# Moving columns of 256 and 512 in pairs of 64-byte lines: another order inside each matmul of a two-layer block

## The chip, the core and the metric

The kernel runs on one core of one Trainium2 chip. The metric is the device time of one execution in microseconds, from the first to the last of the core's work. Engines are named as in the profile: PE is TensorE's matmuls, PEld its loads of the stationary operand (weight loads), DVE is VectorE, ACT is ScalarE, POOL is GpSimd, SP issues most of the transfers.

## What is computed

Two transformer-like layers run one after the other on 256 tokens of width 2048, in float32. The first has sparse attention and a gated linear recurrence side by side, with 16 tokens put in front (so 272 rows); the second has a long convolution and grouped attention side by side, and then a feed-forward part of width 5632. Cut to what matters here:

```python
# first layer, 272 rows
proj = rms_norm(x, norm_g) @ w_in                      # 2048 -> 12,368
merged = sum_n(sigmoid(gates_n) * (y_n @ w_branch_n))  # attention and recurrence
x = x + merged @ w_out
# second layer, 256 rows
proj = rms_norm_2(x, mix_norm_g) @ w_in
merged = g_h * (y_h @ w_br_hyena) + g_a * (y_a @ w_br_attn)
x = x + merged @ w_out
h2 = rms_norm_2(x, ffn_norm_g)
return x + (silu(h2 @ w_ffn_gate) * (h2 @ w_ffn_up)) @ w_ffn_down
```

Nearly all of the arithmetic is in these products with weight matrices, which are read once each (393 MB from memory).

## The kernel before

**Splitting.** Products are made in a reduced float32 form (`float32r`). To keep float32's accuracy each operand is split in two parts, high and low, and a product is three matmuls: high by high, high by low, low by high. A weight matrix comes from memory in units into `raw`; ScalarE rounds half a unit into `w_hi` (L815, 128 x 1024 elements) and VectorE makes the rest, `w_lo = raw - w_hi` (L1348). Both have four slots; TensorE counts `half_done` when it has used a half, and ScalarE waits for that before it overwrites a slot. TensorE waits for `split_hi` and `split_lo` ahead of each half.

**Two shapes of product.** Activations are kept transposed, features on the partitions and tokens along the row. In `by_tile` (L2278) a tile of 128 x 128 weights is the stationary operand and a row of tokens moves: 256 columns of `x1t`, `hf_hi`/`hf_lo`, `yh`, `ya_hi`/`ya_lo`, or 272 columns of `h_hi`/`h_lo` in the first layer. Its matmuls are at L2285 (high weights) and L2290 (low weights). In `chunk` (L2330) and in the down projection (L2969 on, `down_step`) 128 tokens are stationary and 512 columns of `w_hi` or `w_lo` move: these matmuls are in `by_high` (L2275, L2276), at L2359 and at L2976; the very first and very last steps use `product` (L2269 to L2271). The page prints the operands as `ps<-moving,stationary`.

**Where things lie.** A row of 256 float32 columns is 1024 bytes, one of 512 is 2048, one of 272 is 1088. The kernel has constants `LINE, PHASE = 256, 64` (L126) and starts `x1t`, `hf_hi`, `hf_lo`, `y_hi`, `y_lo`, `yh`, `ya_hi`, `ya_lo`, `st_hi` and `st_lo` at an address that is 64 more than a multiple of 256; `w_hi`, `w_lo` and `h_hi` start at 128 more than a multiple of 256. Each result of a matmul of 512 columns fills a bank of PSUM (2 KB of each partition), one of 256 columns half a bank. ScalarE and VectorE read the banks in plain order.

**Order.** Each engine's program is written out by hand, with semaphores between. TensorE runs through the projections, puts the small products of attention, recurrence and convolution in between at fixed steps, and ends with the feed-forward part (L2285 and L2290 with `hf`, 1447 to 1945 us) and the down projection (L2275, L2276, L2976 with `st`, 1945 to 2191 us). One group of small matmuls matters for the prediction: L2568 multiplies by `half_blocks(ql, lev)`, which takes every second block of n = 1, 2, 4, ... 64 columns of a row of 128 (L557), so 64 columns in pieces of n, and writes them side by side.

Of the kernel before, what the change touches and what calls it, by code (L numbers as in the profile page):

```python
# [24 lines left out]
T = 256  # L25
# [38 lines left out]
def hybrid_layers(nc, a, out):  # L64

    ctx = ExitStack()
    with ctx:
# [2196 lines left out]
        @block.tensor  # L2264
        def _(pe):
            def product(dst, left, w_h, w_l, first, last):

                hi, lo = left
                pe.matmul(dst, hi, w_h, start=first, stop=False)  # L2269
                pe.matmul(dst, hi, w_l, start=False, stop=False)  # L2270
                return pe.matmul(dst, lo, w_h, start=False, stop=last)  # L2271

            def by_high(dst, left, w_h, first):

                pe.matmul(dst, left[0], w_h, start=first, stop=False)  # L2275
                pe.matmul(dst, left[1], w_h, start=False, stop=False)  # L2276

            def by_tile(q, h, k0, moving, dsts, last):  # L2278

                pe.wait_ge(split_hi, 8 * q + h + 1)  # L2280
                for e in range(4):
                    for x in range(2):
                        w_h = w_hi[:, h % 4, e // 2, (e % 2) * T + x * P:(e % 2) * T + (x + 1) * P]
                        for i, part in enumerate(moving(k0 + e)):
                            pe.matmul(dsts[x], w_h, part, start=(k0 + e == 0 and i == 0), stop=False)  # L2285
                pe.wait_ge(split_lo, 8 * q + h + 1)
                for e in range(4):
                    for x in range(2):
                        w_l = w_lo[:, h % 4, e // 2, (e % 2) * T + x * P:(e % 2) * T + (x + 1) * P]
                        ins = pe.matmul(dsts[x], w_l, moving(k0 + e)[0], start=False, stop=(k0 + e == last))  # L2290
                ins.then_inc(half_done, 1)
# [38 lines left out]
            def chunk(q, halves, left, dsts, width=W, step=None, new=None, fresh=False):  # L2330

                n = 2 * len(halves)
                for x, h in enumerate(halves):
# [15 lines left out]
                    else:  # L2349
# [6 lines left out]
                        for e in range(2):  # L2356
                            k = 2 * x + e
                            for i, dst in enumerate(dsts):
                                ins = pe.matmul(dst, left(k, i)[0], w_lo[:, h % 4, e, 0:width],  # L2359
                                                start=False, stop=(k == n - 1))  # L2360
# [608 lines left out]
            def down_step(k, par, h, s, outs, first, last):  # L2969
# [5 lines left out]
                for bank, e, cols in outs:  # L2975
                    ins = pe.matmul(ps[bank][:, :], st_hi[:, par, s, cols], w_lo[:, h % 4, e, :], start=False, stop=last)  # L2976
                ins.then_inc(half_done, 1)
# [111 lines left out]
```

## Time and profile before

| | us |
|---|---|
| time, median of 2 runs | 2197.01 (2196.88 to 2197.14) |
| span of the profiled execution, first to last instruction | 2195.1 |
| time around the span (median less span) | 1.9 |
| TensorE matmuls busy | 2188.4, 14295 instructions |
| weight loads busy | 1978.1, 14295 instructions |
| VectorE, ScalarE, GpSimd busy | 1374.6, 1000.1, 359.0 |

The profiled execution has no time of its own beside its span. The page gives the busy time of each engine, then the span in slices, then the chain of work that ended last, followed back from the end. A group of instructions is one line of the kernel with one operation and one pair of operands; behind the bar stand the time in which at least one of the group ran, the mean duration of one in ns, and the idle time of the engine just before. Matmuls overlap in the records, so a duration is longer than the time from one start to the next.

### The profile page before, as it was taken

How to read it: one execution, taken by the hardware profiler on the slowest of the kernel's cores; microseconds unless marked ns; L12 is line 12 of the kernel's file. 1: busy time of each engine (PE TensorE's matmuls, PEld its weight loads, DVE VectorE, ACT ScalarE, POOL GpSimd, SP SyncE). 2: the span in 40 equal slices, each digit the busy share in tenths (PEclk: the TensorE clock that was granted, in tenths of full speed). 3: DMA queues.
4: the chain of work that ended last, by engine and by line, in shares of the span. 5: the costliest groups of instructions: out<-in, count | busy, mean ns of one | idle time of the engine just before them, and what ended most of it. 6: DMA issues, size and time to landing. Idle time of an engine off the chain costs nothing.

```text
span 2195.1 us, 34712 instructions
## 1 busy us (share of the span) xinstructions
PE 2188.4 (100%) x14295; PEld 1978.1 (90%) x14295; DVE 1374.6 (63%) x1873; ACT 1000.1 (46%) x1328; POOL 359.0 (16%) x437
## 2 busy tenths in 40 slices
PE   9999999999999999999999999999999999999999
PEld 7898889988888878899999999899999999988887
DVE  6777557968575576677775546555555555554444
ACT  6446544253444446555544444454344333444443
POOL 6563999760000000000000000000000000000000
PEclk9999999999999999999999999999999999999999
DMA  8655556444465645554455556555555555555553
GB/s 274 196 168 176 181 172 189 145 154 153 154 212 198 214 156 171 171 182 145 157 189 173 192 173 194 190 186 182 189 190 179 185 191 183 182 190 192 178 190 129
DMA packets 276530, 396.63 MB, mean 181 GB/s; under 512 B 9399, under 2 KB 198162, under 8 KB 270896
## 3 DMA queue, kind: packets, MB, share of 16 engines
q1 hardware_dynamic: 272704, 384.52, 53.4%
q0 software_dynamic: 3648, 10.37, 1.8%
q8 instruction: 81, 1.33, 0.2%
q14 instruction: 33, 0.27, 0.0%
q10 hardware_dynamic: 64, 0.14, 0.0%
HBM read 392.91 MB, written 2.10 MB: 180 GB/s over the span
## 4 chain that ended last, share of the span: by engine, by line
PE 98%; DVE 1%; DMA 0%; ACT 0%; SPq 0%; issue 0%; DVEq 0%
PE ps L2285 32%; PE ps L2290 16%; PE ps L2275 15%; PE ps L2276 15%; PE ps L2359 11%; PE ps L2976 4%; PE ps L2568 1%; PE ps L2318 0%; PE ps L2515 0%; DMA raw<-w_in 0%; PE ps L2475 0%; PE ps L2791 0%; PE ps L2851 0%; PE ps L2811 0%; PE ps L2837 0%; PE ps L2724 0%
## 5 line engine op out<-in xcount | busy, mean ns | idle before, releaser
L1348 DVE TENSOR_TENSOR w_lo<-raw,w_hi 128x1024 fp32r<-128x1024 f32 x719 | 893.7, 1250 | 630.4 <-ACT w_hi L815 624.6
L815 ACT ACTIVATE w_hi<-raw 128x1024 fp32r<-128x1024 f32 x719 | 751.3, 1057 | 732.2 <-PE ps L2290 446.3
L2285 PE MATMUL ps<-hf_hi,w_hi 128*128 128x256 f32 x1408 | 339.4, 281 | 0.0
L2285 PE MATMUL ps<-hf_lo,w_hi 128*128 128x256 f32 x1408 | 339.1, 281 | 0.0
L2285 PEld LDWEIGHTS ps<-hf_lo,w_hi 128*128 128x128 f32 x1408 | 266.4, 189 | 0.1
L2285 PEld LDWEIGHTS ps<-hf_hi,w_hi 128*128 128x128 f32 x1408 | 265.8, 189 | 0.1
L2275 PE MATMUL ps<-w_hi,h_hi 128*128 128x512 f32 x572 | 232.9, 407 | 0.6 <-DVE h_lo L1403 0.6
L2285 PE MATMUL ps<-x1t,w_hi 128*128 128x256 f32 x1792 | 232.1, 282 | 0.0
L2276 PE MATMUL ps<-w_hi,h_lo 128*128 128x512 f32 x572 | 224.8, 393 | 0.0
L2285 PEld LDWEIGHTS ps<-x1t,w_hi 128*128 128x128 f32 x1792 | 218.5, 189 | 1.9 <-issue 1.4
L2290 PE MATMUL ps<-hf_hi,w_lo 128*128 128x256 f32 x1408 | 194.3, 281 | 0.0
L2290 PEld LDWEIGHTS ps<-hf_hi,w_lo 128*128 128x128 f32 x1408 | 178.1, 189 | 0.0
L2359 PE MATMUL ps<-w_lo,h_hi 128*128 128x512 f32 x572 | 155.3, 393 | 0.0
L2275 PE MATMUL ps<-w_hi,st_hi 128*128 128x512 f32 x348 | 138.3, 397 | 0.0
L2276 PE MATMUL ps<-w_hi,st_lo 128*128 128x512 f32 x348 | 138.3, 397 | 0.0
L2359 PEld LDWEIGHTS ps<-w_lo,h_hi 128*128 128x128 f32 x572 | 107.4, 188 | 24.7
L2275 PEld LDWEIGHTS ps<-w_hi,h_hi 128*128 128x128 f32 x572 | 107.5, 188 | 23.3 <-DVE h_lo L1403 0.8
L2276 PEld LDWEIGHTS ps<-w_hi,h_lo 128*128 128x128 f32 x572 | 107.8, 188 | 21.8
L2290 PE MATMUL ps<-x1t,w_lo 128*128 128x256 f32 x896 | 123.0, 280 | 0.0
L2290 PEld LDWEIGHTS ps<-x1t,w_lo 128*128 128x128 f32 x896 | 112.9, 189 | 0.0
L2285 PE MATMUL ps<-h_hi,w_hi 128*128 128x272 f32 x384 | 100.7, 295 | 0.0
L2285 PE MATMUL ps<-h_lo,w_hi 128*128 128x272 f32 x384 | 98.4, 288 | 0.0
(512 smaller groups left out, 3122.4 us busy)
## 6 DMA issues: line engine op xcount, KB each, us to landing
raw<-w_in SPq DMA_DIRECT2D x163, 1024.0 KB, 5.2
raw<-w_ffn_gate SPq DMA_DIRECT2D x44, 1024.0 KB, 5.1
raw<-w_ffn_up SPq DMA_DIRECT2D x44, 1024.0 KB, 5.1
raw<-w_ffn_down SPq DMA_DIRECT2D x44, 1024.0 KB, 4.9
raw<-w_out SPq DMA_DIRECT2D x32, 1024.0 KB, 5.1
raw<-w_branch SPq DMA_DIRECT2D x16, 1024.0 KB, 5.1
raw<-w_br_hyena SPq DMA_DIRECT2D x8, 1024.0 KB, 5.8
raw<-w_br_attn SPq DMA_DIRECT2D x8, 1024.0 KB, 5.8
```

The lines of the kernel that those rows point to most:

```text
L815: act.activation(w_hi[:, h % 4, :, 0:width], raw[:, h // 2, 2 * (h % 2):2 * (h % 2) + 2, 0:width], ACT.Copy).then_inc(split_hi, 1)
L1348: dve.tensor_tensor(w_lo[:, h % 4, :, 0:width], raw[:, h // 2, 2 * (h % 2):2 * (h % 2) + 2, 0:width], w_hi[:, h % 4, :, 0:width].bitcast(F ...
L2275: pe.matmul(dst, left[0], w_h, start=first, stop=False)
L2276: pe.matmul(dst, left[1], w_h, start=False, stop=False)
L2285: pe.matmul(dsts[x], w_h, part, start=(k0 + e == 0 and i == 0), stop=False)
L2290: ins = pe.matmul(dsts[x], w_l, moving(k0 + e)[0], start=False, stop=(k0 + e == last))
L2359: ins = pe.matmul(dst, left(k, i)[0], w_lo[:, h % 4, e, 0:width], start=False, stop=(k == n - 1))
L2568: ins = pe.matmul(ps[6 + c][0:rows, i * (P // 2):(i + 1) * (P // 2)].rearrange("p (k n) -> p k n", n=2 ** (lev - 1)), kl[:, i, c * P:c * P ...
L2976: ins = pe.matmul(ps[bank][:, :], st_hi[:, par, s, cols], w_lo[:, h % 4, e, :], start=False, stop=last)
```

## The change

TensorE's matmuls read a row of 256 or 512 moving columns in another order and write their results in the same order, so each result lands where it did before. A row is cut in two halves and each half in pieces of 16 columns (64 bytes); piece 0 of the first half is followed by piece 0 of the second half, then come piece 1 of both, and so on to the last pair. Inside a piece the order is plain. The two pieces of a pair are 512 bytes apart for 256 columns, 1024 bytes for 512. It is done by an access pattern of three dimensions (pair, half, column) in place of one, on the moving operand and on the result; stationary operands, instructions, waits and transfers stay. Rows of any other length (the 272 of the first layer, the narrow ones) are left as they were: `sweep` returns them unchanged.

```diff
+            def sweep(x):
+
+                return x.rearrange("p (a j s) -> p j a s", a=2, s=16)[:, :, :, :] if x.shape[1] in (T, W) else x
+
             def product(dst, left, w_h, w_l, first, last):
 
                 hi, lo = left
+                dst, w_h, w_l = sweep(dst), sweep(w_h), sweep(w_l)
                 pe.matmul(dst, hi, w_h, start=first, stop=False)
...
             def by_high(dst, left, w_h, first):
 
+                dst, w_h = sweep(dst), sweep(w_h)
                 pe.matmul(dst, left[0], w_h, start=first, stop=False)
                 pe.matmul(dst, left[1], w_h, start=False, stop=False)
...
                         for i, part in enumerate(moving(k0 + e)):
-                            pe.matmul(dsts[x], w_h, part, start=(k0 + e == 0 and i == 0), stop=False)
+                            pe.matmul(sweep(dsts[x]), w_h, sweep(part), start=(k0 + e == 0 and i == 0), stop=False)
...
-                        ins = pe.matmul(dsts[x], w_l, moving(k0 + e)[0], start=False, stop=(k0 + e == last))
+                        ins = pe.matmul(sweep(dsts[x]), w_l, sweep(moving(k0 + e)[0]), start=False, stop=(k0 + e == last))
...
-                                ins = pe.matmul(dst, left(k, i)[0], w_lo[:, h % 4, e, 0:width],
+                                ins = pe.matmul(sweep(dst), left(k, i)[0], sweep(w_lo[:, h % 4, e, 0:width]),
                                                 start=False, stop=(k == n - 1))
...
-                    ins = pe.matmul(ps[bank][:, :], st_hi[:, par, s, cols], w_lo[:, h % 4, e, :], start=False, stop=last)
+                    ins = pe.matmul(sweep(ps[bank][:, :]), st_hi[:, par, s, cols], sweep(w_lo[:, h % 4, e, :]),
+                                    start=False, stop=last)
```

## Rows read from the trace of the kernel before

**Rows 1.** The page: busy time, granted TensorE clock by slice, chain by engine.
```profile
PE 2188.4 (100%) x14295; PEld 1978.1 (90%) x14295; DVE 1374.6 (63%) x1873; ACT 1000.1 (46%) x1328; POOL 359.0 (16%) x437
...
PEclk9999999999999999999999999999999999999999
...
PE 98%; DVE 1%; DMA 0%; ACT 0%; SPq 0%; issue 0%; DVEq 0%
```
**Rows 2.** Waits of TensorE, longest first: us in total, times, longest us.
```profile
PE ps L2420 <- DVE junk L1394: 1.5, 1, 1.5
```
**Rows 3.** Groups by line, PE, 1600 to 1650 us: count | busy us, mean ns | idle.
```profile
L2285 PE MATMUL ps<-hf_lo,w_hi 128*128 128x256 f32 x144 | 34.7, 281 | 0.0
L2285 PE MATMUL ps<-hf_hi,w_hi 128*128 128x256 f32 x144 | 34.7, 281 | 0.0
L2290 PE MATMUL ps<-hf_hi,w_lo 128*128 128x256 f32 x139 | 19.5, 281 | 0.0
```
**Rows 4.** The same view of 1456 to 1471 us.
```profile
L2285 PE MATMUL ps<-hf_lo,w_hi 128*128 128x256 f32 x46 | 10.7, 276 | 0.0
L2285 PE MATMUL ps<-hf_hi,w_hi 128*128 128x256 f32 x46 | 10.7, 276 | 0.0
L2290 PE MATMUL ps<-hf_hi,w_lo 128*128 128x256 f32 x43 | 5.9, 276 | 0.0
```
**Rows 5.** The same view of 2000 to 2050 us.
```profile
L2276 PE MATMUL ps<-w_hi,st_lo 128*128 128x512 f32 x72 | 28.6, 397 | 0.0
L2275 PE MATMUL ps<-w_hi,st_hi 128*128 128x512 f32 x72 | 28.6, 397 | 0.0
L2976 PE MATMUL ps<-w_lo,st_hi 128*128 128x512 f32 x72 | 19.8, 397 | 0.0
```
**Rows 6.** Line L2276 alone: durations min/median/max in ns, first and last start.
```profile
L2276 PE MATMUL ps<-w_hi,h_lo x572: 387/393/403, 12.8 to 718.0; 128*128 128x512 f32 x191
...
L2276 PE MATMUL ps<-w_hi,st_lo x348: 397/397/398, 1945.1 to 2187.3; 128*128 128x512 f32 x174
...
L2276 PE MATMUL ps<-w_hi,x1t x224: 387/392/398, 848.7 to 1445.9; 128*128 128x512 f32 x112
```
**Rows 7.** Line L2290 alone, in the same columns.
```profile
L2290 PE MATMUL ps<-hf_hi,w_lo x1408: 276/281/281, 1448.8 to 1944.8; 128*128 128x256 f32 x176
...
L2290 PE MATMUL ps<-h_hi,w_lo x384: 283/288/296, 118.1 to 442.3; 128*128 128x272 f32 x192
```
**Rows 8.** Groups by line over the whole span, PE, one row of each pattern.
```profile
L2285 PE MATMUL ps<-hf_hi,w_hi 128*128 128x256 f32 x1408 | 339.4, 281 | 0.0
...
L2275 PE MATMUL ps<-w_hi,h_hi 128*128 128x512 f32 x572 | 232.9, 407 | 0.6 <-DVE h_lo L1403 0.6
L2285 PE MATMUL ps<-x1t,w_hi 128*128 128x256 f32 x1792 | 232.1, 282 | 0.0
...
L2275 PE MATMUL ps<-w_hi,st_hi 128*128 128x512 f32 x348 | 138.3, 397 | 0.0
...
L2290 PE MATMUL ps<-x1t,w_lo 128*128 128x256 f32 x896 | 123.0, 280 | 0.0
...
L2275 PE MATMUL ps<-w_hi,x1t 128*128 128x512 f32 x224 | 88.7, 396 | 0.0
```
**Rows 9.** Timeline, PE, around 391, 423 and 439 us: start, us, xcount.
```profile
390.14 1.28 PE L2568 MATMUL ps<-ql,kl 128*128 128x64 f32 x10
...
422.08 1.28 PE L2568 MATMUL ps<-ql,kl 128*128 128x64 f32 x10
...
438.21 1.15 PE L2568 MATMUL ps<-ql,kl 128*64 128x64 f32 x16
```
**Rows 10.** Line L2837 alone: plain float32, 512 columns, the slowest here.
```profile
L2837 PE MATMUL ps<-zt,t_cos x8: 590/592/595, 1059.7 to 1087.0; 128*128 128x512 f32 x8
```
**Rows 11.** Groups by line, all engines, 1600 to 1650 us: the two splitters.
```profile
L1348 DVE TENSOR_TENSOR w_lo<-raw,w_hi 128x1024 fp32r<-128x1024 f32 x18 | 22.0, 1225 | 23.1 <-ACT w_hi L815 22.9
...
L815 ACT ACTIVATE w_hi<-raw 128x1024 fp32r<-128x1024 f32 x18 | 19.1, 1059 | 30.9 <-PE ps L2290 30.9
```

## The prediction

> **What bounds the kernel now.** I read the page first. TensorE is busy for the whole span, its granted clock is full in every slice, and the chain of work that ended last is 98% TensorE [rows 1]. The view of waits then shows that TensorE hardly waits: its largest wait is 1.5 us in total [rows 2]. So the time is the number of matmuls times the pace at which they follow one another, and nothing else has to be late for a change of that pace to show in full.
>
> The pace can't be read off the duration in a group, because a record's end is modelled; it has to be counted. A view of one stretch counts every matmul that touches it, so those begun up to one duration before it come off. In 50 us of the feed-forward part there are 144 + 144 + 139 = 427 records of 281 ns, less 2.4 for the edge: 50/424.6 = 117.8 ns [rows 3]. In another stretch the same instructions show 276 ns and 46 + 46 + 43 = 135 records in 15 us: 15/132.6 = 113.1 ns [rows 4]. In the down projection there are 3 x 72 = 216 records of 397 ns in 50 us: 233.3 ns [rows 5]. Record less pace is 163 ns all three times. From here on I read the pace of any steady group as its duration less 163.
>
> At 2.4 GHz, the granted level, 256 columns alone would be 106.7 ns and 512 columns 213.3 ns. So a matmul of 256 loses 11 ns, one of 512 some 17 ns (229 to 233), though no wait is recorded. That loss is what an order of columns could touch.
>
> What sets it? Three observations. The same instruction runs at 276 or 281 and keeps to it for long stretches [rows 3, 4]. With the same moving tile, `w_hi`, a matmul of 512 shows 392 or 393 where the weights loaded meanwhile are of `x1t` or `h_lo` and 397 where they are of `st_lo` [rows 6], so the loading of the next weights has a part in it. And where rows start 64 bytes further round each time (the 272 columns of `h_hi` are 1088 bytes, against the 256 bytes that the kernel's LINE names), records spread from 283 to 296; rows of 256 columns, which all start at the same place, show 276 to 281 [rows 7]. I read this as two readers, the moving stream and the load of the next weights, that get in each other's way depending on which 64-byte line of four each is at. That reading is an inference; no view shows a collision.
>
> **The change part by part.** Nothing is added or removed: the same matmuls, weight loads, waits and transfers. Only the order changes in which columns are read and results written. Matmuls of 256 columns that go the new way: 3 x 1408 with `hf`, 1792 + 896 with `x1t`, and 768 with `yh` and `ya`: 7680. Of 512 columns: 3 x 572, 3 x 348, 3 x 224, 6 x 128 with `y` and `hf`, and 24 at the first and last steps: 4224 [rows 8], which has one row of each pattern. The 272-column ones stay. That is 7680 x 117.6 = 903 us and 4224 x 230.6 = 974 us, 1877 of the span of 2195.1. In pieces of 16 columns it is 122,880 + 135,168 = 258,048 jumps.
>
> *A jump in reading.* The matmuls at L2568 already read broken rows: at the first level 64 columns come as 64 pieces of one column, at the fifth as 4 pieces of 16. Both go at (1.28 - 0.27)/9 = 112 ns; at the last level 64 columns in one piece, with half the weights, go at 62 ns or less [rows 9]. So 112 ns is the pace of loading 128 weights, and 64 jumps hide in the 50 ns between: a jump costs at most 0.8 ns, at least nothing. Over all pieces the upper end is 206 us. I take nothing, since 60 jumps more make no difference between the two levels.
>
> *A jump in writing.* No matmul of the trace writes a broken row of PSUM, so nothing prices it from a row nearby. The bound below is nothing, as each piece is 16 results side by side. The bound above is the slowest 512 columns here: 592 - 163 = 429 ns, 1.9 times the pace now [rows 10]. I take nothing, because the broken reads showed nothing. The Trainium skill speaks against that: "Advanced Engine Details and Errata", section Memory Cachelines, says that any non-contiguous pattern in PSUM slows matmuls significantly, but also that two neighbours side by side give the best throughput, which pieces of 16 satisfy. By its first sentence the time would be that of the fourth rival below, by its second nothing is lost.
>
> *The meeting with the weight load.* A weight load passes 512 bytes, eight 64-byte lines, in 112 ns: 14 ns a line. The moving stream now passes one in 117.8/16 = 7.4 ns, twice as fast, so the two meet at changing places. With pairs 512 or 1024 bytes apart, both whole multiples of 256, the stream stays two pieces long at each of the four places and then goes on: 14.7 ns a place, the speed of the load. If both walk the same way they keep in step and hardly meet; if the load runs the other way round, they meet for longer each time. No row tells the direction. From below, the quickest paces that rows show: 113.1 for 256 and 387 - 163 = 224 for 512 [rows 4, 6], a gain of 7680 x 4.5 + 4224 x 6.6 = 35 + 28 = 63 us; if all loss went, 256 would still stand at the load's 112 ns and 512 at 213.3, a gain of 43 + 73 = 116 us. From above, meeting twice as often doubles the loss: 7680 x 11 + 4224 x 17.3 = 84 + 73 = 157 us. Between such ends I take the steady paces that rows show at mixed places. The 272 rows at 288 - 163 = 125 ns are 117.6 for 256 columns, today's pace; the few stretches that run quick now lose 4.5 ns, some 450 matmuls, 2 us; 512 goes to the steady 233.3, which costs the 3180 matmuls that aren't of the down projection 3.6 ns each, 11 us. Sum: +13 us.
>
> *What lies behind TensorE.* If it got quicker the splitters would have to keep up. In the 50 us of the feed-forward part VectorE splits 18 halves in 22.0 us and waits 23.1 us for ScalarE, which itself waits 30.9 us for TensorE [rows 11]. Both have room for 5%, so a gain would not be eaten there.
>
> The sum goes on the span, 2195.1 us; the median, 2197.0, has 1.9 us around it. 2197 + 13 = 2210 us, +0.6%.
>
> **Rivals.** *In step:* the stream and the load walk the same way and the pace falls to the quick one. For it: 276-ns records exist and last [rows 4]. Against it: the start of rows is already laid out (LINE, PHASE), and the direction is unknown. 2197 - 63 = 2134 us; it decides from 256 at 114.5 and 512 at 226 on. This ends on the other side, faster by over 2%.
>
> *Against the load:* the two walk opposite ways and each meeting lasts longer. For it: the spread of 13 ns in the 272 rows [rows 7] shows that places alone can cost that much. Against it: whoever is held up once is out of step with the other for a while. Half the doubled loss is 79 us, 2276 us; all of it 2354. It decides once 256 takes over 121 ns and 512 over 236.
>
> *No difference at all:* the order inside a row does not matter, the loss being per 64-byte line whatever line comes next (11 ns is 16 lines x 0.7). Then 2197 us; it falls in the same band as my forecast.
>
> *Broken writes are slow:* matmuls go at the 429 ns per 512 columns of rows 10, 1.9 times the pace. 1877 x 0.87 = 1630 us more, about 3830 us. Nothing in the rows speaks for it.
>
> **How the numbers follow.** 2% of 2197 is 44 us, about what a measurement of this kernel can tell from no change. About the same, with no difference included (2153 to 2241): 0.42. In step, faster: 0.20. Against the load, slower: 0.33. Slow writes: 0.05. So faster 0.20, same 0.42, slower 0.38. The forecast is the likeliest, 2210 us, with 2153 to 2241 as its own range. For 8 in 10 the range takes in the whole middle, the in-step case at the paces that rows already show (2134, so down to 2130), and the against case up to about three quarters of the doubled loss (2197 + 113 = 2310). Outside stay a full loss removed (2081), the loss doubled and the slow writes.
>
> **What would show it.** The page after must again be 98% TensorE in its chain, with the full clock and as many matmuls; else a step has become a wait that I don't see. Records of 256 columns near 281 to 283 and of 512 near 397 bear out the sum. 276 and 387 or less are in step; 284 and over with 400 and over is against the load; 600 and over for 512 columns is slow writes. The 272-column rows, which don't change, must stay at 283 to 296: if they move too, it isn't the order. If 256 and 512 move in opposite ways, the reading with two walkers is right in kind and my price for one of them wrong. I would be wrong in kind if the weight loads, 188 ns now, grew: then it is the load that is held up and not the stream.

## The result: slower, 2254.44 us, and the profile after

The changed kernel takes 2254.44 us (median of 2 runs, 2254.37 to 2254.52) against 2197.01: ratio 1.0261 [1.0242, 1.0279]. That is 57 us more where the prediction had 13 more, inside its wide range and outside the likeliest case's own (2153 to 2241).

The page after: busy times, the clock by slice and the chain by engine, which answer to [rows 1].

```profile
PE 2246.4 (100%) x14295; PEld 2009.5 (89%) x14295; DVE 1375.1 (61%) x1873; ACT 1001.2 (44%) x1328; POOL 352.7 (16%) x437
...
PEclk9999999999999999999999999999999999999999
...
PE 99%; DVE 0%; DMA 0%; ACT 0%; SPq 0%; issue 0%; DVEq 0%
```

As many matmuls, the same clock, still a chain of matmuls alone. No wait was added: the matmuls themselves follow one another more slowly. Groups by line, PE only, in 50 us of the feed-forward part (1650 to 1700) and of the down projection (2050 to 2100); they answer to [rows 3] and [rows 5] (the change moved the lines by 6).

```profile
L2291 PE MATMUL ps<-hf_hi,w_hi 128*128 128x256 f32 x142 | 34.9, 284 | 0.0
L2291 PE MATMUL ps<-hf_lo,w_hi 128*128 128x256 f32 x141 | 34.6, 283 | 0.0
L2296 PE MATMUL ps<-hf_hi,w_lo 128*128 128x256 f32 x136 | 19.1, 283 | 0.0
...
L2281 PE MATMUL ps<-w_hi,st_hi 128*128 128x512 f32 x71 | 28.6, 402 | 0.0
L2282 PE MATMUL ps<-w_hi,st_lo 128*128 128x512 f32 x70 | 28.2, 402 | 0.0
L2982 PE MATMUL ps<-w_lo,st_hi 128*128 128x512 f32 x69 | 19.5, 402 | 0.0
```

142 + 141 + 136 = 419 matmuls of 256 columns, less 2.4 for the edge, are 50/416.6 = 120.0 ns; 71 + 70 + 69 = 210 of 512 columns, less 1.7, are 50/208.3 = 240.0 ns. Record less pace is still 163. The single lines, minimum/median/maximum in ns, which answer to [rows 6] and [rows 7]:

```profile
L2282 PE MATMUL ps<-w_hi,h_lo x572: 402/403/407, 12.8 to 735.9; 128*128 128x512 f32 x191
L2282 PE MATMUL ps<-w_hi,st_lo x348: 402/402/403, 1995.6 to 2244.7; 128*128 128x512 f32 x174
L2282 PE MATMUL ps<-w_hi,x1t x224: 402/402/407, 871.6 to 1485.9; 128*128 128x512 f32 x112
...
L2296 PE MATMUL ps<-hf_hi,w_lo x1408: 282/284/289, 1489.1 to 1995.2; 128*128 128x256 f32 x176
...
L2296 PE MATMUL ps<-h_hi,w_lo x384: 283/288/296, 121.4 to 450.2; 128*128 128x272 f32 x192
```

Three things are to be seen. The 272 columns, which the change leaves alone, stand where they stood, so it is the order. The 512 columns of `h_lo`, `st_lo` and `x1t`, which differed before (393, 397, 392), are now all alike. And the new paces are round: 120.0 is 106.7 + 16 x 0.83 and 240.0 is 213.3 + 32 x 0.83, as much as if every 64-byte line of a moving row cost 0.83 ns, one cycle of 1.2 GHz, above the bare columns.

Counted from the starts of all matmuls in the two traces, the changed ones of 256 columns took 906.0 us before and 926.2 after, those of 512 columns 989.0 and 1026.3, everything else 294.6 and 294.6. The two differences, 20.3 and 37.3, are the 57.5 us by which the span grew.

### The profile page after: what moved, and what is told of

The parts are those of the page before. It is cut to its first block, busy times and chain, and to the rows that moved or that the text cites. A ratio compares the mean times of both kernels' runs of the same rounds, so it can differ in the third digit from the quotient of the medians.

```text
span 2252.6 us, 34712 instructions
## 1 busy us (share of the span) xinstructions
PE 2246.4 (100%) x14295; PEld 2009.5 (89%) x14295; DVE 1375.1 (61%) x1873; ACT 1001.2 (44%) x1328; POOL 352.7 (16%) x437
## 4 chain that ended last, share of the span: by engine, by line
PE 99%; DVE 0%; DMA 0%; ACT 0%; SPq 0%; issue 0%; DVEq 0%
PE ps L2291 31%; PE ps L2296 16%; PE ps L2281 15%; PE ps L2282 15%; PE ps L2365 11%; PE ps L2982 4%; PE ps L2574 1%; PE ps L2324 0%; PE ps L2521 0%; DMA raw<-w_in 0%; PE ps L2481 0%; PE ps L2857 0%; PE ps L2797 0%; PE ps L2817 0%; PE ps L2843 0%; PE ps L2730 0%
## 5 line engine op out<-in xcount | busy, mean ns | idle before, releaser
L2291 PE MATMUL ps<-hf_hi,w_hi 128*128 128x256 f32 x1408 | 345.9, 284 | 0.0
L2291 PE MATMUL ps<-hf_lo,w_hi 128*128 128x256 f32 x1408 | 345.4, 283 | 0.0
L2281 PE MATMUL ps<-w_hi,h_hi 128*128 128x512 f32 x572 | 237.9, 416 | 0.6 <-DVE h_lo L1403 0.6
L2291 PE MATMUL ps<-x1t,w_hi 128*128 128x256 f32 x1792 | 237.7, 286 | 0.0
L2282 PE MATMUL ps<-w_hi,h_lo 128*128 128x512 f32 x572 | 230.4, 403 | 0.0
L2291 PEld LDWEIGHTS ps<-x1t,w_hi 128*128 128x128 f32 x1792 | 223.8, 190 | 1.9 <-issue 1.4
L2365 PE MATMUL ps<-w_lo,h_hi 128*128 128x512 f32 x572 | 160.5, 403 | 0.0
```

The lines of the kernel that those rows point to most:

```text
L2291: pe.matmul(sweep(dsts[x]), w_h, sweep(part), start=(k0 + e == 0 and i == 0), stop=False)
L2365: ins = pe.matmul(sweep(dst), left(k, i)[0], sweep(w_lo[:, h % 4, e, 0:width]), start=False, stop=(k == n - 1))
```

## The experiments

### Results apart from reads

Which half of the change costs: `sweep` stays on the moving operand alone, or on the result alone.

```diff
-                dst, w_h = sweep(dst), sweep(w_h)
+                dst, w_h = plain(dst), sweep(w_h)        # reads only; plain(x) returns x
+                dst, w_h = sweep(dst), plain(w_h)        # writes only
...
```

Reads only:

> Only the moving operand is read in pairs; results are written in plain order (so columns of each product change places, which alters the values but not the work). Theory A and B (reading is what costs): 120 and 240 ns, about 2254 us. Theory C (writing costs): the paces of before, 113 to 118 and 226 to 233, about 2197 us.

Writes only:

> Only the results are written in pairs; the moving operand is read in plain order (columns of each product change places, the work is the same). Theory A and B: the paces of before, about 2197 us. Theory C (writing costs): 120 and 240 ns, about 2254 us.

Reads only took 2254.42 us, ratio 1.0261 [1.0240, 1.0281]; writes only 2196.96 us, ratio 0.9999 [0.9989, 1.0009]. Groups by line of the kernel that only writes in the new order (1650 to 1700 and 2050 to 2100 us, one row of each):

```profile
L2295 PE MATMUL ps<-hf_hi,w_hi 128*128 128x256 f32 x142 | 34.3, 281 | 0.0
...
L2286 PE MATMUL ps<-w_hi,st_lo 128*128 128x512 f32 x72 | 28.6, 397 | 0.0
```

281 and 397 are the records of the kernel before [rows 3, 5]. The whole price is in the read; 64-byte pieces half a row apart cost nothing when written to PSUM.

### Other orders, same pieces

The first edit takes the pairs from the last to the first, the second exchanges neighbouring pieces (1, 0, 3, 2, ...); both keep every jump.

```diff
-                return x.rearrange("p (a j s) -> p j a s", a=2, s=16)[:, :, :, :] ...
+                return x.rearrange("p (a j s) -> p j a s", a=2, s=16)[:, ::-1, :, :] ...    # last to first
+                return x.rearrange("p (j a s) -> p j a s", a=2, s=16)[:, :, ::-1, :] ...    # neighbours
```

> The same pairs, taken from the last pair to the first; inside a piece of 16 columns the order stays plain. The changed kernel shows 120.0 ns for 256 columns and 240.0 for 512, that is 0.83 ns over the streaming time for every piece of 16, whatever weights are loaded. Theory A (a jump has a fixed price of 0.83 ns, wherever it goes and whatever the weight load does): 120 and 240 again, about 2254 us. Theory B (the stream walks against the weight load): turned round it walks with it, the meetings go, 256 columns fall to 112 to 114 ns and 512 to 214 to 226, so 2050 to 2140 us. Theory C (the broken writes cost it): as A, about 2254 us.

> Another order with a jump after every piece: the row goes in pieces of 16 columns with neighbours exchanged (1, 0, 3, 2, ...), so successive pieces never share their place modulo 256 bytes. Theory A (fixed price of a jump): 120 and 240 ns, about 2254 us. Theory D (the price is for two pieces in succession at the same place modulo 256 bytes): paces like those before the change, 113 to 118 and 226 to 233, 2140 to 2200 us. Theory B (against the load): somewhere between the two, with a spread over matmuls that the flat 240 of the changed kernel doesn't have.

From last to first took 2188.84 us, ratio 0.9963 [0.9949, 0.9977]: quicker than the changed kernel and than the kernel before. Neighbours exchanged took 2234.96 us, 1.0172 [1.0155, 1.0189]. Groups by line in the down projection (2050 to 2100 us) and the feed-forward part (1650 to 1700), first from last to first, then neighbours exchanged:

```profile
L2282 PE MATMUL ps<-w_hi,st_lo 128*128 128x512 f32 x74 | 28.8, 389 | 0.0
...
L2291 PE MATMUL ps<-hf_lo,w_hi 128*128 128x256 f32 x142 | 34.2, 280 | 0.0
```

```profile
L2282 PE MATMUL ps<-w_hi,st_lo 128*128 128x512 f32 x71 | 28.3, 398 | 0.0
...
L2291 PE MATMUL ps<-hf_lo,w_hi 128*128 128x256 f32 x142 | 34.9, 284 | 0.0
```

As many jumps, backward, are free: from start to start the 512 columns with `st` follow one another at 228 ns, under the 233 of before, those of 256 at 117. (389 less 163 would be 226: between orders the difference of record and pace moves by some 2 ns.) So there is no fixed price of a jump. Theory D falls as well: neighbours exchanged never put two pieces at the same place one after the other, and yet 256 columns went at 120.0 ns, where 113 to 118 were expected, and 512 with `st` at 235.5. Direction counts, as the theory of two walkers said, but the size it gave (2050 to 2140 us) was far off: the 256 columns gained nothing (906.0 us in all, as before), the 512 columns 8.3 us. Whether the load of weights had any part in it was left to the next runs.

### Is it the load of the next weights?

Some matmuls load only 32 of their 128 stationary columns: the second moving part of every product, and the low ones that don't close a sum. This is done to the changed order, the plain order and the order from last to first.

```diff
-                pe.matmul(dst, left[1], w_h, start=False, stop=False)
+                pe.matmul(dst[0:32], left[1][:, 0:32], w_h, start=False, stop=False)
```

> The changed kernel's order, but the matmuls of the second moving part, and the low matmuls that don't close a sum, load only 32 of their 128 stationary columns (and so fill 32 of 128 result rows: this part of the computation is left out); the moving columns are as many as before. The load that lies beside a matmul is then a quarter as long wherever the next matmul is one of these. Theory Load (the 0.83 ns per 64-byte piece comes from the moving read meeting the load of the next weights): beside a short load 256 columns fall from 120 to 107 to 110 ns and 512 from 240 to 213 to 222; beside a full load they stay 120 and 240. Theory Order alone (the pieces of the forward order cost 0.83 ns each whatever the load does): 120 and 240 beside short and full loads alike.

> The order of the kernel before, with the same matmuls cut to 32 stationary columns (the same part of the computation left out). Theory Load: the loss of the plain order is of the same kind, so beside a short load 256 columns fall from 113 to 118 to about 107 to 110 ns, and 512 from 229 to 233 to 213 to 218. Theory Order alone, with the plain order's loss coming from the read too: 113 to 118 and 229 to 233 as in the kernel before. If the plain order falls and the forward pairs of e5 don't, the two losses are of different kinds.

> The pairs from last to first, as in e1, with the same matmuls cut to 32 stationary columns (the same part of the computation left out). Theory Load: beside a short load 107 to 110 and 213 to 218 ns, the same as the other two orders, since the order matters only through the load. Theory Order alone: 113 to 121 and 226 to 231 as in e1, and other than e5 by the same 2.6 and 11 ns as with full loads.

The times, one run each: changed order 2253.03, plain 2169.86, from last to first 2187.44 us, beside 2197.15 of the kernel before on the same chip. Groups by line of the changed order, 2050 to 2100 us, matmuls and then weight loads, and one row of 1650 to 1700:

```profile
L2281 PE MATMUL ps<-w_hi,st_hi 128*128 128x512 f32 x70 | 28.2, 403 | 0.0
L2282 PE MATMUL ps<-w_hi,st_lo 128*32 128x512 f32 x70 | 28.2, 403 | 0.0
...
L2281 PEld LDWEIGHTS ps<-w_hi,st_hi 128*128 128x128 f32 x69 | 13.1, 190 | 8.9
L2282 PEld LDWEIGHTS ps<-w_hi,st_lo 128*32 128x32 f32 x69 | 7.7, 112 | 3.4
...
L2292 PE MATMUL ps<-hf_hi,w_hi 128*128 128x256 f32 x138 | 33.9, 283 | 0.0
```

The load beside `st_hi`'s matmul, that of the next weights, took 191 ns in the changed kernel and takes 112 here, by the records; the matmul is at 403, against 402. The changed order pays its 0.83 ns a line beside the short load too: theory Load falls for it. The plain order in the same two stretches:

```profile
L2282 PE MATMUL ps<-w_hi,st_lo 128*32 128x512 f32 x72 | 28.4, 394 | 0.0
...
L2292 PE MATMUL ps<-hf_hi,w_hi 128*128 128x256 f32 x149 | 34.7, 277 | 0.0
```

Here the load has a share: 256 columns fall from 281 to 277, about 4 of the 11 ns that they lose (the quick stretches of [rows 4] stood at 276), 512 columns with `st` only from 397 to 394 to 396. The order from last to first hardly moved (2188.84 and 2187.44 us). So two things had been taken for one: a small share of the load, which the plain order of 256 columns has, and a loss of the read by itself, which stays without it.

### One walk backward, and pieces of other sizes

One walk from the last piece to the first; then pieces of 32 columns, forward and backward; pieces of 8; and even pieces before odd ones.

```diff
+                return x.rearrange("p (j s) -> p j s", s=16)[:, ::-1, :] ...                    # one walk backward
+                return x.rearrange("p (a j s) -> p j a s", a=2, s=32)[:, :, :, :] ...           # 128 bytes
+                return x.rearrange("p (a j s) -> p j a s", a=2, s=32)[:, ::-1, :, :] ...        # 128 bytes, backward
+                return x.rearrange("p (a j s) -> p j a s", a=2, s=8)[:, :, :, :] ...            # 32 bytes
+                return x.rearrange("p (j a s) -> p a j s", a=2, s=16)[:, :, :, :] ...           # even, then odd
```

> One walk instead of two: pieces of 16 columns, no pairs, from the last piece to the first, columns plain inside a piece, results written alike. Theory Load (the load runs against a forward read): a single walk backward runs the way of the load at twice its speed, meets it about a third as often as the plain order and stays longer: between the backward pairs and the plain order, 2180 to 2200 us, 256 columns 113 to 118, 512 columns 226 to 232. Theory Order alone, price for any piece that is not the next line forward: e1 already speaks against that, 2254 us. Theory Pairs (it is going back and forth between two halves that costs, the direction only in the change of half): about 2197 us.

> The order of the changed kernel with pieces of 32 columns (128 bytes) in place of 16. e5 to e7 showed that the price does not come from the weight load, so it lies in the order of reading alone. Theory Piece (the first 64 bytes of every piece wait one cycle of 1.2 GHz, 0.83 ns, what follows in line goes on at full pace): 256 columns are 8 pieces, 106.7 + 6.7 = 113.3 ns, 512 are 16, 213.3 + 13.3 = 226.7 ns; 2254 - 7680 x 6.7 - 4224 x 13.3 = 2147 us, below the kernel before. Theory Line (every 64-byte line pays in a pair order, however long the piece): 120 and 240, 2254 us. Theory Plain inside (inside a piece the plain order's own loss of about half a cycle a line, at its start one cycle): 256 columns 113.3 + 8 x 0.42 = 117 ns, 512 columns 226.7 + 16 x 0.5 = 235 ns, about 2205 us.

> Pairs of 128-byte pieces from last to first. Theory Piece: as the forward pairs of 128 bytes or quicker, 113 and 227 at most, 2147 us or less. Theory Line: as e1, 117 and 229, 2189 us. Theory Plain inside: between e1 and the kernel before, 2189 to 2197 us.

> Forward pairs of pieces of 8 columns (32 bytes), so that each 64-byte line is opened twice. Theory Piece: 256 columns are 32 pieces, 106.7 + 26.7 = 133.3 ns, 512 are 64, 266.7 ns; 2254 + 7680 x 13.3 + 4224 x 26.7 = 2469 us. Theory Line, where a line that was left can be returned to for nothing: 120 and 240, 2254 us. If the two lines of a pair hold each other up at each change: 266.7 and more.

> No pairs: first the even pieces of 16 columns from first to last, then the odd ones, so each piece starts 128 bytes after the one before, and never at the next line. Theory Piece: 120 and 240, 2254 us, as with the pairs. If only pieces that are a multiple of 256 bytes apart hold each other up (pairs, half a row apart): near the plain order or below, 113 to 118 and 227 to 233, 2147 to 2197 us.

| order | us | ratio | 256 columns, ns | 512 columns (`st_hi`), ns |
|---|---|---|---|---|
| one walk backward | 2223.47 | 1.0119 [1.0102, 1.0136] | 117.8 | 237.5 |
| pairs of 128 bytes | 2231.47 | 1.0155 [1.0138, 1.0172] | 118.8 | 238.0 |
| the same, backward | 2230.63 | 1.0151 [1.0134, 1.0168] | 118.7 | 237.1 |
| pairs of 32 bytes | 2279.65 | 1.0374 [1.0353, 1.0394] | 120.2 | 242.5 |
| even, then odd | 2264.81 | 1.0306 [1.0285, 1.0327] | 121.4 | 240.0 |

The paces are means from start to start with `hf` and `st_hi`; in pairs of 32 bytes other tiles of 256 columns took 121.7 to 125.0. Nearly all expectations missed. Pairs of 128 bytes have half the pieces and did not save half the price; 32 bytes have twice the pieces and cost 25 us more instead of 215. One walk backward is slower than either the plain order or the pairs backward. So it is neither a fixed price per piece, nor a fixed one per line, nor one of direction as such.

### The orders by themselves

Behind the last result of the kernel before, groups of 32 matmuls run with everything else idle, one group for each order, width, load and start; the `wide` row is that of `w_hi`.

```diff
             down_last(FKT // 4 - 1, 0)
+            pe.wait_ge(final_ready, 8)
+            for _ in range(32): pe.matmul(ps[0][:, 0:256], st_hi[:, 0, 0, 0:128], wide[:, 0:256], start=True, stop=True)
+            for _ in range(32): pe.matmul(ps[0][:, 0:256].rearrange(...), st_hi[:, 0, 0, 0:128], wide[:, 0:256].rearrange(...), ...)
...
```

> The kernel before, and behind its last result 84 groups of 32 more matmuls each, whose results nobody uses: one moving row of w_hi, one stationary tile of st_hi, while every other engine and nearly every transfer has ended. The groups go through twelve orders (plain; the changed kernel's; from last to first; neighbours exchanged; one walk backward; pairs of 128 bytes, forward and backward; pairs of 32 bytes; even pieces then odd; four walks forward and backward; both indices backward), 256 and 512 columns, 128 and 32 stationary columns, and for three orders other starts of the moving row and of the stationary tile, 64 bytes further each. The time is longer by the groups, 84 x 32 x about 180 ns = 480 us. Theory Order alone (the price lies in how the moving row is read, nothing else of the kernel takes part): the paces of the runs before: plain 113 to 118 and 226 to 233 ns, the changed order 120 and 240, from last to first 115 to 118 and 226 to 230, neighbours exchanged 120 and 235, pairs of 32 bytes 120 to 125 and 243, even then odd 121 and 240. Theory Traffic (ScalarE, VectorE and the transfers write the same memory meanwhile and hold the read up): with these idle all orders go at 107 to 110 and 213 to 218. Theory Load: equal paces of all orders beside 32 stationary columns only; e5 speaks against it. If the start of the row moves the pace of the plain or backward order, but not of the changed one, which 64-byte line of four is read when has a part in it.

The timeline of that part, PE: start in us, us from the first start to the last end, the line (one for each group). The rows are the plain order (L3011), the changed one (L3012) and that from last to first (L3013) for 256 columns, the same three for 512 columns (L3023 to L3025), and the plain and changed order of 256 columns beside 32 stationary columns (L3035, L3036).

```profile
2193.01 4.04 PE L3011 MATMUL ps<-w_hi,st_hi 128*128 128x256 f32 x32 [0.78 <-DVE x L2261]
2196.88 4.01 PE L3012 MATMUL ps<-w_hi,st_hi 128*128 128x256 f32 x32
2200.73 3.90 PE L3013 MATMUL ps<-w_hi,st_hi 128*128 128x256 f32 x32
...
2238.81 7.49 PE L3023 MATMUL ps<-w_hi,st_hi 128*128 128x512 f32 x32
2246.13 7.84 PE L3024 MATMUL ps<-w_hi,st_hi 128*128 128x512 f32 x32
2253.82 7.47 PE L3025 MATMUL ps<-w_hi,st_hi 128*128 128x512 f32 x32
...
2329.36 3.81 PE L3035 MATMUL ps<-w_hi,st_hi 128*32 128x256 f32 x32
2333.01 4.00 PE L3036 MATMUL ps<-w_hi,st_hi 128*32 128x256 f32 x32
```

A group's length less one record, over 31, is its pace: (4.01 - 0.283)/31 = 120.2 ns, (7.84 - 0.403)/31 = 239.9 ns. ScalarE, VectorE and the transfers have stopped, and the paces are those of the whole kernel within some 5 ns (the plain 512 columns with `st_hi` had 233.3 there and have 228.9 here), those of the changed order exactly: theory Traffic falls too. The time was 2670.42 us (one run), the groups included. Means from start to start within a group, the first few left out, with the moving row where it is and then 64, 128 and 192 bytes further:

| | 256 columns, ns | 512 columns, ns |
|---|---|---|
| changed order | 120.0, 120.3, 120.0, 120.0 | 240.0, 240.0, 240.0, 240.0 |
| plain | 117.8, 118.9, 113.5, 119.8 | 228.9, 233.2, 233.4, 227.5 |
| from last to first | 116.5, 116.7, 117.4, 120.7 | 228.3, 228.3, 226.7, 233.4 |

Other starts of the stationary tile moved the plain and the backward order in the same way (512 columns plain 226.8 to 233.4, backward 228.3 to 236.8) and the changed one not at all (120.0, 240.0 to 240.1). The plain order depends on the start: it pays as for half of its lines (113.3 = 106.7 + 8 x 0.83, 226.7 = 213.3 + 16 x 0.83) up to nearly all. The changed order always pays as for all. In no group, here or in the later runs, did the mean come below half. Beside 32 stationary columns the plain order of 256 columns goes at 113.3 here too; but with the moving row 128 bytes further it goes at 113.5 beside a full load as well, so what the load costs it depends on the start, and 512 columns gain nothing by the short load (231.1 against 228.9). Of the paces expected, those of neighbours exchanged were missed (117.8 and 233.3 in place of 120 and 235); one walk backward, for which none had been named, took 120.0 for 256 columns, against 117.8 in the kernel.

### Step and distance, one at a time

Again behind the kernel before: pieces of 16 columns at a fixed step of 1 to 8 lines, forward and backward, and pairs 16 to 32 lines apart, forward and backward.

```diff
+            for _ in range(24): pe.matmul(..., flat[:, 0:1024].rearrange("p (n d s) -> p n d s", n=16, s=16)[:, :, 0, :], ...)           # step 4
+            for _ in range(24): pe.matmul(..., flat[:, 0:544].rearrange("p (a j s) -> p j a s", a=2, s=16)[:, 0:8, :, :], ...)           # pairs 17 apart
```

> As the run of orders alone, with 120 groups of 24 matmuls behind the last result of the kernel before. A moving row is now 16 or 32 pieces of 16 columns out of all four slots of w_hi. Either each piece starts a fixed number of 64-byte lines after the one before (1 to 8, forward and backward), or pieces go in pairs that are 16, 17, 18, 19, 20, 24 or 32 lines apart, from the first pair on and from the last pair on; beside 128 and 32 stationary columns. Longer by 120 x 24 x about 180 ns = 520 us. Theory Same place (a piece waits for the one just before when both stand at the same of four 64-byte places of 256 bytes): steps of 4 and 8, either way, 120 and 240 ns or more; pairs 16, 20, 24 and 32 apart 120 and 240, pairs 17 and 19 apart less, 113 to 118 and 227 to 236. Theory Rhythm (which of four places stand where in the sequence decides, and order alone; nothing else of the distance): steps of 1, 5, -3 and -7 alike, -1, -5, 3 and 7 alike, 2 and 6 as even then odd, 120 and 240; pairs 16, 20, 24 and 32 apart alike. Theory Distance (any piece that is not the next line waits): every step but 1 at 120 and 240, pairs too, backward too; the runs from last to first speak against it.

The time was 2706.90 us (one run). Timeline rows of pairs 16, 17, 18, 19, 20, 24 and 32 lines apart, forward, 512 columns, 128 stationary columns (start, length):

```profile
2369.52 5.92 PE L3057 MATMUL ps<-w_hi,st_hi 128*128 128x512 f32 x24
2375.28 5.92 PE L3058 MATMUL ps<-w_hi,st_hi 128*128 128x512 f32 x24
2381.04 6.08 PE L3059 MATMUL ps<-w_hi,st_hi 128*128 128x512 f32 x24
2386.95 6.00 PE L3060 MATMUL ps<-w_hi,st_hi 128*128 128x512 f32 x24
2392.79 5.92 PE L3061 MATMUL ps<-w_hi,st_hi 128*128 128x512 f32 x24
2398.55 5.92 PE L3062 MATMUL ps<-w_hi,st_hi 128*128 128x512 f32 x24
2404.31 5.92 PE L3063 MATMUL ps<-w_hi,st_hi 128*128 128x512 f32 x24
```

5.92 less 0.40 over 23 is 240 ns: pairs 16, 20, 24 and 32 apart go alike, 18 apart is the slowest at 246.7. The same for the steps, mean ns from start to start, 128 stationary columns:

| step in lines | 256 columns | 512 columns |
|---|---|---|
| 1 and 5 | 117.7, 117.8 | 229.1, 228.9 |
| 2 and 6 | 122.2, 122.3 | 238.5, 238.6 |
| 3 and 7 | 120.0, 119.8 | 233.3, 236.6 |
| 4 and 8 | 122.1, 121.7 | 239.8, 240.0 |
| -1 and -5 | 120.2, 120.0 | 237.9, 237.9 |
| -2 and -6 | 119.9, 120.0 | 237.3, 237.4 |
| -3 and -7 | 118.6, 118.7 | 232.5, 232.5 |
| -4 and -8 | 122.0, 122.0 | 240.0, 240.0 |

Steps that differ by four lines, 256 bytes, go alike (3 and 7 differ by 3 ns at 512 columns and not at 256): theory Distance falls, a step of 5 lines costs no more than the plain order. Theory Same place falls as a rule of neighbours only: steps of 4 pay for every line, as it said, but pairs 17 apart, which it wanted quick, stand at 121.4 and 240.0, and 18 apart, which never repeat a place within two pieces, at 120.0 and 246.7. Pairs from the last on are cheap when 16, 20, 24 or 32 apart (228.3 to 228.4 for 512) and dear when 17 apart (240.0). Theory Rhythm, the sequence of the four places, fits best, with misses beside a full load. A step of -3 is not quite that of 1 (232.5 against 229.1 for 512 columns); -1 and -5 stand at 237.9, where 3 and 7 have 233.3 and 236.6; 2 and 6 took 122.2 and 122.3 for 256 columns in place of 120; and backward pairs of 256 columns 16 apart took 116.4, those 20, 24 and 32 apart 113.3.

The same run has these groups beside 32 stationary columns, and there the steps with the same sequence of places come together. For 512 columns, 1, 5, -3 and -7 go at 231.0 to 231.7 ns, 3, 7, -1 and -5 at 233.3 to 233.4, 2 and 6 at 239.8 and 240.2, -2 and -6 at 242.3, and 4, 8, -4 and -8 at 243.3 to 243.4. So the sequence of places ranks the orders, and a full load moves single steps by up to 5 ns, up or down. Pairs 16, 20, 24 and 32 apart, from the first on, stay at 240.0 beside both.

### One partition's read, or all of them

The same groups behind the kernel before, with fewer partitions (rows of the product) and fewer stationary columns.

```diff
+            for _ in range(24): pe.matmul(ps[0][0:128, 0:256], st_hi[0:64, 0, 0, 0:128], wide[0:64, 0:256], start=True, stop=True)
+            for _ in range(24): pe.matmul(ps[0][0:4, 0:256], st_hi[0:32, 0, 0, 0:4], wide[0:32, 0:256], start=True, stop=True)
```

> As the runs of orders alone, with 60 groups of 24 matmuls behind the last result of the kernel before: the plain order, the changed one, the one from last to first, one walk backward, and pieces that are all at the same place of 256 bytes (a step of four lines); 256 and 512 columns; products over all 128 partitions, over 64 and over 32 of them; 128 and 4 stationary columns. Longer by 60 x 24 x about 180 ns = 260 us. Theory Rows collide (partitions read the same line one after the other, and those further down meet those further up at a place, so the rhythm of the places counts): over 32 partitions the price is gone or much smaller, 256 columns at 107 to 110 and 512 at 213 to 218 with 4 stationary columns in all orders. Theory Reader (each partition's own read loses the cycle, whatever the others do): the paces of e13 and e14 whatever the number of partitions: 120 and 240 for the changed order, 121 to 122 and 240 to 243 for the step of four. Theory Load: with 4 stationary columns in place of 32 the plain and backward orders fall further, the changed order doesn't.

The time was 2513.80 us (one run). Leaving out groups in which the clock changed, all paces but two over 64 partitions lie within 0.3 ns of those over 128: the changed order 120.0 and 240.0 again, one walk backward 120.0 and 237.9. The two are 512 columns beside a full load, from last to first (228.3 against 233.4) and with the step of four (240.0 against 243.4); the runs before had them at 228.3 and 239.8 over all 128, so one and the same group can settle at either pace, as the 276 and 281 ns of [rows 3, 4] did. A difference of some 5 ns between two single groups of 512 columns therefore proves little, except for the changed order, which never left 240.0. During the groups over 32 partitions the granted clock fell. First the timeline of the first starts of the changed order over 32 partitions, still at full clock; then the windows view (window, its length, then busy us and counts of PE, PEld, DVE, ACT and POOL, granted clock, DMA share, GB/s) over groups of 64, 32, and again 128 and 64 partitions:

```profile
2224.78 0.76 PE L3023 MATMUL ps<-w_hi,st_hi 32*128 32x256 f32 x5
...
2275.00:2303.00 28.00, 28.00 (x120) 21.85 (x119) 0.00 (x0) 0.00 (x0) 0.00 (x0) 1.00 0.00 1
2312.00:2351.00 39.00, 39.00 (x93) 29.66 (x92) 0.00 (x0) 0.00 (x0) 0.00 (x0) 0.50 0.00 0
2413.00:2463.00 50.00, 50.00 (x213) 17.64 (x212) 0.00 (x0) 0.00 (x0) 0.00 (x0) 1.00 0.00 0
```

And the timeline of four orders at the low clock, 512 columns over 32 partitions (changed, from last to first, one walk backward, step of four):

```profile
2311.07 10.44 PE L3038 MATMUL ps<-w_hi,st_hi 32*128 32x512 f32 x24
2321.31 10.44 PE L3039 MATMUL ps<-w_hi,st_hi 32*128 32x512 f32 x24
2331.55 10.44 PE L3040 MATMUL ps<-w_hi,st_hi 32*128 32x512 f32 x24
2341.79 10.44 PE L3041 MATMUL ps<-w_hi,st_hi 32*128 32x512 f32 x24
```

(0.76 - 0.278)/4 = 120 ns: the changed order pays the same over a quarter of the partitions. Theory Rows falls, and theory Reader fits; no run tells each partition's own read from something that is done once for all of them. At 1.2 GHz (clock 0.50) every order goes at (10.44 - 0.623)/23 = 427 ns, which is 512 columns at that clock and nothing else. So the price exists only at the full clock: a line then has 6.7 ns, and with the added cycle takes 7.5; at the low clock it has 13.3 ns, and no order pays. The plain float32 matmuls of [rows 10] agree: at the full clock they take 429 ns for 512 columns, 13.4 ns a line, and hardly more than 427. That the time for a line is what counts is argued, not shown.

The changed order over 128 partitions with 4 stationary columns, 256 and 512 columns:

```profile
2356.51 3.04 PE L3043 MATMUL ps<-w_hi,st_hi 128*4 128x256 f32 x24
...
2412.76 5.92 PE L3058 MATMUL ps<-w_hi,st_hi 128*4 128x512 f32 x24
```

(3.04 - 0.28)/23 = 120 ns and (5.92 - 0.40)/23 = 240 ns: it stays where it was. The plain order of 256 columns stands at 113.4, no lower than beside 32 (113.3), where theory Load wanted a further fall.

## Why the prediction was right and wrong

**What bounds the kernel: right.** The time is matmuls times pace, no wait took part, and 20.3 + 37.3 us of pace are the whole difference. Record less 163 gave the paces after as well, at both widths, and those of the other orders within some 2 ns.

**A jump in writing at nothing: right, by luck.** Writes alone have 0.9999 [0.9989, 1.0009], so "Broken writes are slow" falls. The reason given, that the broken reads showed nothing, was none: a read says nothing of a write, and for reads it was no evidence either, as the next paragraph says. The sentence of the Trainium skill that spoke against it ("Advanced Engine Details and Errata", section Memory Cachelines: any non-contiguous pattern in PSUM slows matmuls significantly) does not hold for pieces of 64 bytes here; the measurement decides.

**A jump in reading at nothing: wrong in its evidence.** It rested on L2568 [rows 9], whose pace of 112 ns is the weight load's. 64 columns need at most 62 ns there, so a loss in reading of up to 50 ns hid under the load, and "60 jumps make no difference" was a statement about the load. These rows are also plain float32, like [rows 10]: a 64-byte line has 13.4 ns in them, about what it has at the low clock, where no order paid. So they might have shown no loss even without the load; no run tests that. The bound drawn from them, 0.8 ns a jump, held: 57.5 us over 258,048 jumps are 0.22 ns each. But it isn't a price of jumps. The changed order stands 0.83 ns a line above bare columns, and of that the plain order was already paying a part, 0.68 ns a line for 256 columns (10.9/16) and about 0.54 for 512 (17.3/32). The change adds only what is missing to 0.83: 2.4 ns and 9.4 ns a matmul, 7680 x 2.4 + 4224 x 9.4 = 18 + 40 = 58 us.

**The meeting with the weight load, +13 us: the step that failed.** Its sign came out; its sizes did not. It took the steady paces that the rows before show, 117.6 and 233.3 ns, for those at which any mixed order settles. So it put 2 us on the 256 columns, 11 on the 512 outside the down projection (3.6 ns each) and nothing on the down projection; 20.3, 30.2 (9.5 ns each) and 7.0 us were measured, at 120.0 and 240.0 ns. And for the changed order its mechanism fell. That the plain order's loss depends on where rows and weights start was read rightly from [rows 4, 6, 7], as the runs of orders alone show, and the load has a share of it in 256 columns (281 to 277 with short loads). From this I took the whole loss to be meetings. The changed order keeps to 120.0 and 240.0 with 128, 32 and 4 stationary columns, at every start (120.3 at one), and with every other engine idle; half that loss or more is in the plain order too, whatever is loaded.

**"Against the load" was nearest in numbers and not in kind.** Its marks were records of 284 and over and 400 and over; 283 to 284 and 402 came. Its time was 2276, its condition 121 and 236 ns, and 120 and 240 were measured. Its sentence "for it", the spread of the 272 columns, was the better evidence: in the runs of orders alone the start by itself moves the plain 256 columns from 113.5 to 119.8. But "half the doubled loss" was no mechanism's size: the changed order stands at one cycle a line, which with 16 and 32 lines gives 120 and 240. That is no ceiling, as other orders went to 123.3 and 246.7. **"No difference at all"** had the unit right (so much per 64-byte line, "11 ns is 16 lines x 0.7") and missed that an order can move it, from half the lines to all of them and beyond. **"In step"** fell for the changed order; the pairs from last to first, which it would have called the other direction, gained 8 us, not 63.

**The marks.** The 272 columns stayed at 283 to 296, as they had to. The weight loads did grow, 189 to 191 in the down projection, which the prediction named as the sign of being wrong in kind (before, then after, 2050 to 2100 us):

```profile
L2276 PEld LDWEIGHTS ps<-w_hi,st_lo 128*128 128x128 f32 x72 | 13.6, 189 | 3.2
...
L2282 PEld LDWEIGHTS ps<-w_hi,st_lo 128*128 128x128 f32 x71 | 13.6, 191 | 3.5
```

Short loads show that the load is not what holds the matmul: the short load takes 111 to 112 ns beside the changed order and 107 to 109 beside the two others, so it is itself slowed a little.

**What stays open:** what in the read of the moving row loses the cycle. For the changed order the runs exclude the results, other engines and transfers, the distance of a pair beyond its remainder by 256 bytes, the number of partitions and the load. They show that the order of reading is the cause, that the sequence of the four 64-byte places ranks the orders better than any other theory tried, that the loss ends with the full clock, and that the plain and the backward order also move with the stationary tile's start. Why a rising pair order pays as for every line and a falling one in most groups for fewer (113.3 to 120.7 and 226.7 to 236.8 ns) isn't explained by any run.

## What to carry to other kernels

The order in which a matmul reads its moving row is a setting of its own: here, in `float32r` at the full clock, the loss was 0.4 to 1.0 ns a 64-byte line, by order and start, though no wait shows it. Try the order from last to first beside the intended one, and judge by the records of a steady stretch: here one gave 2.6% more, the other 0.4% less than the plain order. Before a cost is put at nothing because a row of the trace doesn't show it, ask what sets the pace of that row; a group that waits for its weights can't price a read.

## What the runs showed that I had not expected

- Many steady paces at the full clock are the bare columns and a whole number of cycles of 1.2 GHz: 8 and 16 more in 113.3 and 120.0 ns for 16 lines, 16, 24 and 32 more in 226.7, 233.3 and 240.0 for 32 (not all: 117.8 ns is 13.4 more). The lowest in any run pays as for half the lines; the slowest, pairs 18 lines apart, pays 1.25 cycles a line (246.7 ns).
- At 1.2 GHz the four orders timed there don't differ at all: 427 ns for 512 columns in each.
- The clock was granted at 0.50 during matmuls over 32 partitions, with TensorE busy throughout, and rose to 1.00 again during matmuls over 128.
- Results in 64-byte pieces, 512 or 1024 bytes apart in PSUM, cost nothing: 2196.96 against 2197.12 us.
